# Fifteen short matmuls at the head of units in a one-core hybrid encoder layer

## The chip, the cores and the metric

The kernel runs on one core of a Trainium2 chip, all in float32 (matmul operands in the reduced form fp32r). The metric is the device time of one execution in microseconds. TensorE has two granted clock levels, 1.2 and 2.4 GHz.

## The reference

One layer of a chunk-causal encoder trunk on x (1, 256, 2048) and 256 memory tokens. Three residual sub-layers follow one another:

```python
x = x + hybrid_mixer(rmsnorm(x, norm_mix), w_in, ...)          # w_in: 2048 -> 14 parts
x = x + memory_cross_attention(rmsnorm(x, norm_xa), rmsnorm(mem, norm_mem), wq, wkv, wo, gq, gk)
x = x + conv_glu_ffn(rmsnorm(x, norm_ffn), w_up, w_conv, w_down)   # 2048 -> 2 x 5632 -> 2048

# hybrid_mixer:
(qkv_a, a_pre, b_pre, z_a, q_b, k_b, v_b, i_b, f_b, o_b, q_c, k_c, v_c, gate_pre) = split(h @ w_in)
y_a = gated_deltanet(...)      # 6 heads, chunks of 64
y_b = mlstm(...)               # 4 heads
y_c = stick_breaking(...)      # 6 heads
merged = gate_a * (y_a @ wb_a) + gate_b * (y_b @ wb_b) + gate_c * (y_c @ wb_c)
return merged @ w_out
```

Nearly all the work is products of the 256 tokens with weight matrices that are used once each.

## The kernel before

Every weight matrix is walked in units of 256 output columns by all 2048 input rows. STREAM names the phases and their number of units, in order: A 9, Z 3, GA 14, BQK 4, BV 2, BO 2, CQK 6, CV 3, GB 4, GC 6 (all from w_in), BR 8 (w_br), WO 8, K 8, Q 8, V 8, XO 8, UP 44, DN 32. A unit falls into two halves of 128 output columns; this text writes GC0.0 and GC0.1 for the first and second half of GC's first unit. A half is one accumulation over 16 steps of k.

For each half, SP loads the raw float32 weights, ACT splits off a high part into `w_hi_home` (line 547), DVE writes the remainder to `w_lo_home` (line 1139, in `lo_half`), and PE multiplies. Both weight tiles have two slots, one per half, so ACT may write the next high part of a half's slot when PE has finished with it (semaphore `half_used`), and PE may start a half when DVE has finished it (`lo_ready`). The activations stand in `x_hl` in the same way as a high and a low part; x_hl lies in `x_home`.

`three` (lines 1970 to 1972) is one step of k: high weights by high activations, high weights by low activations, low weights by high activations. Each of the three is a weight load of 128 x 128 and a matmul over 256 columns, all into one bank. A half of a phase that is feature-major (weights loaded, tokens moving) is 16 calls of it, 48 matmuls. BV, CV and V are token-major (TM_): the activations are loaded and the weights move, also 48 matmuls a half. UP takes another form (lines 2009 and 2011): a matmul over 512 columns and one over 256 in each step, and so does DN (lines 2485 and 2486).

The order of TensorE's work is written out by hand in one program. `half_unit` is a half with its waits, `product_half(m)` the half number m of the whole stream, `project(name)` a stretch of whole units (units 0 and 1 written out, the rest in a loop of pairs). Where the rest of the layer needs TensorE, its transposes and small products stand between two halves: between the halves of GA the DeltaNet's triangular solve and state, in CQK the mLSTM, in GB the stick-breaking attention, in WO3 transposes of the memory tokens (line 2053), in V the cross-attention. `norm_beside` runs eight halves and puts one product over 256 columns, with a tile of ones, in the middle of the fourth; it is called at WO4.0 and at K0.1. The first four halves of Q have such a product (line 2380) behind every second of them, up to Q3.1. The stretches from GC0.0 to WO2.1, from Q4.0 to Q7.1 and from XO1.0 to XO7.1 consist of halves alone. Every half's results go to columns of a bank that ACT or DVE then evacuate.

Of the kernel before, what the change touches and what calls it, by code (L numbers as in the profile page):

```python
# [8 lines left out]
P = 128  # L9
SEQ, D = 256, 2048  # L10
TT = SEQ // P
KC = D // P
# [10 lines left out]
BIG = 1e30  # L23
W_AT = 24
W_OF = {"UP": 0, "DN": 0, "V": 16}


def place_of(name):
    return W_OF.get(name, W_AT)

# [13 lines left out]
LEVELS, FIRST_LEVEL = 7, 4  # L44
BS = 1 << FIRST_LEVEL
BLOCKS = 12 * P // BS
FM, TM_, BR, DOWN = "feature-major", "token-major", "branches", "down"
# [15 lines left out]
FIRST, COUNT = {}, {}  # L63
# [62 lines left out]
def build_program(nc, T, out):  # L126
# [3 lines left out]
    with ctx:  # L130
# [8 lines left out]
        w_hi_home = sb("w_hi_home", [P, 2, KC * P + 64], f32r)  # L139
# [11 lines left out]
        x_hl = x_home[:, 8:8 + 2 * KC * SEQ].rearrange("p (j k s) -> p j k s", j=2, k=KC)  # L151
# [39 lines left out]
        y_hl = sb("y_hl", [P, 2, KC, SEQ], f32r, b_scope)  # L191
# [343 lines left out]
        def up_bank(par, half):  # L535

            return bank[4 + 2 * par + half]
# [1427 lines left out]
        def _(pe):  # L1965
            mm = nc.tensor.matmul

            def three(o, w, x, start, stop):
# [2 lines left out]
                mm(o, w[0], x[1], start=False, stop=False)  # L1971
                return mm(o, w[1], x[0], start=False, stop=stop)  # L1972

            def wait_bank(name, i):

                if isinstance(i, int) and i < 2:
                    u = FIRST[name] + i - 2
                    if u < 0:
                        return
                    before = phase_of(u)  # L1980
                    e, n = evacuated(before, u - FIRST[before])
                    pe.wait_ge(evac[e], n)
                else:
                    e, n = evacuated(name, 0)
                    pe.wait_ge(evac[e], i + (n - 2))

            def half_unit(name, i, par, hp, half, acts, ready=None, passed=None, parts=None, ks=range(KC)):

                kind = kind_of[name]
                whole = hp * 4 + (2 * par + half + 1)  # L1990
                pe.wait_ge(*((wp_l, parts) if parts else (lo_ready, whole)))
                if kind == TM_:
                    for k in range(KC // 2):
                        kk = half * (KC // 2) + k
                        at = place_of(name) + k * CW
                        w = [t[:, half, at:at + CW] for t in (w_hi_home, w_lo_home)]
                        for a in range(TT):
                            x = [acts[:, j, kk, a * P:(a + 1) * P] for j in range(2)]
                            last = three(bank[par + 2 * a][:, 0:CW], x, w, kk == 0, kk == KC - 1)
                else:  # L2000
                    cuts = (0, GH, GH + MH, KC) if kind == BR else (0, KC)
                    for k in range(KC if name == "UP" else 0):
                        if parts and k == KC // 2:
                            pe.wait_ge(lo_ready, whole)
                        if ready and k % ready[2] == 0:
                            pe.wait_ge(ready[0], ready[1] + k // ready[2] + 1)
                        o = up_bank(par, half)
                        at = place_of(name) + k * P
                        mm(o[:, :].rearrange("p (j s) -> p j s", j=2), w_hi_home[:, half, at:at + P], acts[:, :, k, :],  # L2009
                           start=k == 0, stop=False)  # L2010
                        last = mm(o[:, SEQ:2 * SEQ], w_lo_home[:, half, at:at + P], acts[:, 0, k, :], start=False, stop=k == KC - 1)  # L2011
                    for k in ks if name != "UP" else ():
                        if parts and k == KC // 2:
                            pe.wait_ge(lo_ready, whole)
                        if ready and k % ready[2] == 0:
                            pe.wait_ge(ready[0], ready[1] + k // ready[2] + 1)
                        g = sum(k >= c for c in cuts) - 1
                        w = [t[:, half, k * P:(k + 1) * P] for t in (w_hi, w_lo)]
                        last = three(bank[par + 2 * g][:, half * SEQ:(half + 1) * SEQ], w, [acts[:, j, k, :] for j in range(2)],
                                     k == cuts[g], k + 1 == cuts[g + 1])  # L2020
                        if kind == BR and half and k + 1 in cuts[1:3]:
                            last.then_inc(br_t, 1)
                        if passed is not None and k % 2 and k + 1 < KC:
                            last.then_inc(passed, 1)
                if ks[-1] == KC - 1:
                    last.then_inc(half_used, 1)

            def product_half(m, acts=x_hl, ready=None, passed=None, parts=None, ks=range(KC)):

                name, i, par, hp, half = half_of(m)  # L2030
                if half == 0 and ks[0] == 0:
                    wait_bank(name, i)
                half_unit(name, i, par, hp, half, acts, ready, passed, parts, ks)

            def project(name, acts, start=0, stop=None):
                def unit(i, par, hp):
                    wait_bank(name, i)
                    for half in range(2):
                        half_unit(name, i, par, hp, half, acts)

                stop = COUNT[name] if stop is None else stop
                if start < 2:
                    each_unit(pe, name, unit, start, min(2, stop))
                each_unit(pe, name, unit, max(2, start), stop)
# [10 lines left out]

            def norm_beside(k, m, acts):

                product_half(m, acts)
                product_half(m + 1, acts)
                product_half(m + 2, acts)  # L2060
                product_half(m + 3, acts, ks=range(KC // 2))
                pe.wait_ge(n_add, 5 * k)
                mm(bank[3][:, 0:SEQ], ones[:, :], tmp[:, 0, 0:SEQ], start=True, stop=True).then_inc(n_ss, 1)
                product_half(m + 3, acts, ks=range(KC // 2, KC))
                for j in range(4, 8):
                    product_half(m + j, acts)
# [67 lines left out]
            pe.wait_ge(gw_h, 2)  # L2134
            mm(bank[4][:, SEQ:2 * SEQ], fold, gate_sums[:, :], start=True, stop=True).then_inc(row_mm, 1)
            for m in range(4, 14):
                product_half(m)
            pe.wait_ge(row_v, ROW_V)
            for a in range(TT):
                nc.tensor.transpose(bank[5][:, a * P:(a + 1) * P], rt[:, a * P:(a + 1) * P], ident[:, :])  # L2140
# [49 lines left out]
            pe.wait_ge(qk_e, 6)  # L2190
            chunk_pairs(kk_t, bank[2:5], GH)
            product_half(m + 5)
            product_half(m + 6)
            m += 7
            for _ in range(2 * FIRST_LEVEL - 1):
                product_half(m)
                m += 1
            pe.wait_ge(rows, 160)
            for l in range(FIRST_LEVEL, LEVELS):
# [72 lines left out]
            for j in range(3):  # L2272
                to_features(bank[3 + j], j, lambda h, a: S_T[:, a * GH + h, :], y_t)

            for name in ("BQK", "BV", "BO"):
                project(name, x_hl)


            def scores(b, k, q):
# [67 lines left out]
            product_half(m + 7)  # L2347


            project("GC", x_hl)  # L2350
            pe.wait_ge(y_lo, 4)
            project("BR", y_hl)

            m = first_half("WO")
            product_half(m, x_hl, (m_lo, 0, 2))
# [101 lines left out]
            product_half(m, x_hl, (xo_l, 0, 2), ks=range(4, KC))  # L2457
            product_half(m + 1, x_hl)

            project("XO", x_hl, 1, COUNT["XO"] - 1)  # L2460
            m = first_half("UP")
            product_half(m - 2, x_hl)
            product_half(m - 1, x_hl, None, x_free)
# [75 lines left out]
```

## Time and profile before

| what | value |
|---|---|
| three runs | 1995.47, 2001.36, 2000.78 us (median 2000.78) |
| the profiled execution | 2001.66 us |
| its span in the profile | 1999.8 us, 34706 instructions |
| PE (matmuls) busy | 1985.7 us (99%) |
| PEld (weight loads) busy | 1895.3 us (95%) |
| DVE busy | 1216.7 us (61%) |
| ACT busy | 891.6 us (45%) |
| DMA, mean over the span | 191 GB/s |

The span runs from the first to the last instruction; the execution's own time is 1.9 us longer. Matmuls are pipelined: one matmul's record lasts longer than the step to the next, so the pitch is read from starts or from counts in a stretch, and busy time does not tell it. In a window a matmul that overlaps its edge is counted too.

### The profile page before, as it was taken

Reading aid. Unit: us, or ns where it says so; the run is one execution under the profiler, and the core shown is the slowest. Engines: PE = TensorE matmul, PEld = TensorE weight load, DVE = VectorE, ACT = ScalarE, POOL = GpSimd, SP = SyncE. Lnnn points to the kernel's source line nnn. Section 1 sums busy time; section 2 is a strip of 40 time slices with the busy share of each in tenths; the row PEclk is TensorE's granted clock in tenths of the full one; section 3 lists DMA queues with packets and bytes.
Section 4 is the critical chain, followed back from the end, with each engine's and each line's share of the span. In section 5 each row is a group of like instructions: output and inputs, shape, how many; then the busy total and the mean of one; then the engine's idle time right before and its main releaser. Section 6 shows DMA issues by size and latency. Waiting matters only on the chain.

```text
span 1999.8 us, 34706 instructions
## 1 busy us (share of the span) xinstructions
PE 1985.7 (99%) x14790; PEld 1895.3 (95%) x14790; DVE 1216.7 (61%) x1352; ACT 891.6 (45%) x877; POOL 40.3 (2%) x62
## 2 busy tenths in 40 slices
PE   8999999999999999999999999999999999999999
PEld 8999999999999999999999999888888888888888
DVE  5677645445454476676655345777777777754444
ACT  5445434434374333455434444544444444433333
POOL 1000100000000000000000000000000000000000
PEclk9999999999999999999999999999999999999999
DMA  8665744665557756565554455665656565567564
GB/s 268 212 200 196 226 159 143 211 198 169 181 167 267 238 190 217 177 196 170 191 187 127 151 165 190 214 207 173 204 174 204 175 202 176 176 205 223 185 203 134
DMA packets 356636, 382.65 MB, mean 191 GB/s; under 512 B 8143, under 2 KB 351603, under 8 KB 355123
## 3 DMA queue, kind: packets, MB, share of 16 engines
q1 hardware_dynamic: 350947, 353.36, 55.3%
q0 software_dynamic: 5584, 27.70, 3.9%
q8 instruction: 88, 1.44, 0.3%
q14 instruction: 17, 0.14, 0.0%
HBM read 367.47 MB, written 13.58 MB: 191 GB/s over the span
## 4 chain that ended last, share of the span: by engine, by line
PE 98%; DVE 1%; ACT 0%; DMA 0%; issue 0%; SPq 0%; DVEq 0%; ACTq 0%
PE bank L1970 19%; PE bank L1971 18%; PE bank L1972 18%; PE bank L2009 16%; PE bank L2011 8%; PE bank L2485 8%; PE bank L2486 4%; PE bank L2392 1%; PE bank L2411 1%; PE bank L2169 1%; DVE w_lo_home L1139 0%; PE bank L2215 0%; PE bank L2072 0%; PE bank L2163 0%; DMA ident<-in_shape_masks 0%; PE bank L2281 0%
## 5 line engine op out<-in xcount | busy, mean ns | idle before, releaser
L1139 DVE TENSOR_TENSOR w_lo_home<-raw,w_hi_home 128x2048 fp32r<-128x2048 f32 (+1 forms) x349 | 757.0, 2169 | 604.5 <-ACT w_hi_home L547 604.2
L547 ACT ACTIVATE w_hi_home<-raw 128x2048 fp32r<-128x2048 f32 (+2 forms) x359 | 644.8, 1797 | 1047.0 <-PE bank L1972 627.6
L1970 PE MATMUL bank<-x_home,w_hi_home 128*128 128x256 f32 x2304 | 648.8, 282 | 2.0 <-DVE w_lo_home L1139 1.9
L1972 PE MATMUL bank<-x_home,w_lo_home 128*128 128x256 f32 x2304 | 644.4, 280 | 0.0
L1971 PE MATMUL bank<-x_home,w_hi_home 128*128 128x256 f32 x2304 | 644.4, 280 | 0.0
L2009 PE MATMUL bank<-x_home,w_hi_home 128*128 128x512 f32 x1408 | 488.5, 390 | 0.1
L1970 PEld LDWEIGHTS bank<-x_home,w_hi_home 128*128 128x128 f32 x2304 | 435.1, 189 | 2.9 <-issue 1.4
L1972 PEld LDWEIGHTS bank<-x_home,w_lo_home 128*128 128x128 f32 x2304 | 437.0, 190 | 0.0
L1971 PEld LDWEIGHTS bank<-x_home,w_hi_home 128*128 128x128 f32 x2304 | 433.1, 188 | 0.2
L2011 PE MATMUL bank<-x_home,w_lo_home 128*128 128x256 f32 x1408 | 397.1, 282 | 0.0
L2009 PEld LDWEIGHTS bank<-x_home,w_hi_home 128*128 128x128 f32 x1408 | 264.2, 188 | 55.5 <-issue 0.4
L2011 PEld LDWEIGHTS bank<-x_home,w_lo_home 128*128 128x128 f32 x1408 | 266.5, 189 | 0.0
L2485 PE MATMUL bank<-act_hl,w_hi_home 128*128 128x512 f32 x704 | 245.1, 391 | 0.0
L2486 PE MATMUL bank<-act_hl,w_lo_home 128*128 128x256 f32 x704 | 198.5, 282 | 0.0
L2485 PEld LDWEIGHTS bank<-act_hl,w_hi_home 128*128 128x128 f32 x704 | 132.2, 188 | 27.5
L2486 PEld LDWEIGHTS bank<-act_hl,w_lo_home 128*128 128x128 f32 x704 | 133.2, 189 | 0.0
L1970 PE MATMUL bank<-w_hi_home,mem_hl 128*128 128x256 f32 x256 | 73.6, 287 | 0.0
L1874 DVE SCALAR_TENSOR_TENSOR tmp<-tmp,vec 128x254 f32<-128x254 f32 (+1 forms) x176 | 73.1, 478 | 0.0
L1970 PE MATMUL bank<-mem_hl,w_hi_home 128*128 128x256 f32 x256 | 72.2, 282 | 0.0
L1972 PE MATMUL bank<-mem_hl,w_lo_home 128*128 128x256 f32 x256 | 72.0, 281 | 0.0
L1971 PE MATMUL bank<-mem_hl,w_hi_home 128*128 128x256 f32 x256 | 72.0, 281 | 0.0
L1972 PE MATMUL bank<-y_hl,w_lo_home 128*128 128x256 f32 x256 | 72.0, 281 | 0.0
(315 smaller groups left out, 1946.4 us busy)
## 6 DMA issues: line engine op xcount, KB each, us to landing
raw<-in_w_in SPq DMA_DIRECT2D x52, 2048.0 KB, 8.5
raw<-in_ffn_up SPq DMA_DIRECT2D x44, 2048.0 KB, 7.9
raw<-in_ffn_down SPq DMA_DIRECT2D x32, 1408.0 KB, 6.9
raw<-in_xa_wkv SPq DMA_DIRECT2D x16, 2048.0 KB, 9.2
raw<-in_w_br SPq DMA_DIRECT2D x8, 2048.0 KB, 8.3
raw<-in_w_out SPq DMA_DIRECT2D x8, 2048.0 KB, 8.3
raw<-in_xa_wq SPq DMA_DIRECT2D x8, 2048.0 KB, 8.3
raw<-in_xa_wo SPq DMA_DIRECT2D x8, 2048.0 KB, 8.4
```

The source lines that it names most:

```text
L547: return nc.scalar.activation(out_, in_, func, **kw)
L1139: tt(split_out(w_lo, kind, half, at), halves(raw, kind, half, par), split_out(w_hi, kind, half, at).bitcast(f32), ALU.subtract).then_inc(l ...
L1874: ins = v.scalar_tensor_tensor(o, b, w, o, ALU.mult, ALU.add)
L1970: mm(o, w[0], x[0], start=start, stop=False)
L1971: mm(o, w[0], x[1], start=False, stop=False)
L1972: return mm(o, w[1], x[0], start=False, stop=stop)
L2009: mm(o[:, :].rearrange("p (j s) -> p j s", j=2), w_hi_home[:, half, at:at + P], acts[:, :, k, :], start=k == 0, stop=False)
L2011: last = mm(o[:, SEQ:2 * SEQ], w_lo_home[:, half, at:at + P], acts[:, 0, k, :], start=False, stop=k == KC - 1)
L2169: last = mm(o[:, i * P:(i + 1) * P], lhs(n), rhs(n), start=True, stop=True)
L2392: last = mm(mb(j)[:, 0:SEQ], qT[:, 4 * h + c, a * P:(a + 1) * P], kT[:, 4 * h + c, :], start=c == 0, stop=c == XC - 1)
L2485: mm(o[:, :].rearrange("p (j s) -> p j s", j=2), w_hi_home[:, half, at:at + P], x, start=g + k == 0, stop=False)
L2486: last = mm(o[:, SEQ:2 * SEQ], w_lo_home[:, half, at:at + P], x[:, 0, :], start=False, stop=g * DG + k == FC - 1)
```

## The change

`lead_in` is one extra matmul that starts and stops its own accumulation, with the half's own first weights and activations: with LEAD_WIDE 128 weight columns by 2 tokens, with LEAD_SMALL 4 weight columns by 16 tokens. It is issued behind the half's waits and writes columns of the half's own output, which the first real matmul of the half (start=True) then overwrites. SETTLE is the pair: wide at the head of a unit's first half, small at the head of its second. The pairs go to the units A4 (m = 8, 9), GA3 (m + 6, m + 7), GC0, BR0, WO4, K1 and XO1, and BO0 gets the small one at the head of its first half. Where `project` is now called twice, the order of the halves is as before.

```diff
+LEAD_WIDE, LEAD_SMALL = (P, 2), (4, 16)
+SETTLE = (LEAD_WIDE, LEAD_SMALL)
...
+            def lead_in(o, w, x, shape):
+                m, n = shape
+                return mm(o[0:m, 0:n], w[:, 0:m], x[:, 0:n], start=True, stop=True)
...
-            def half_unit(name, i, par, hp, half, acts, ready=None, passed=None, parts=None, ks=range(KC)):
+            def half_unit(name, i, par, hp, half, acts, ready=None, passed=None, parts=None, ks=range(KC), lead=None):
...
                     cuts = (0, GH, GH + MH, KC) if kind == BR else (0, KC)
+                    if lead:
+                        lead_in(up_bank(par, half)[:, 0:SEQ] if name == "UP" else bank[par][:, half * SEQ:(half + 1) * SEQ],
+                                w_hi_home[:, half, place_of(name):], acts[:, 0, 0, :], lead)
...
             def norm_beside(k, m, acts):
-                product_half(m, acts)
-                product_half(m + 1, acts)
-                product_half(m + 2, acts)
+                leads = dict(zip((m + m % 2, m + m % 2 + 1), SETTLE))
+                for j in range(3):
+                    product_half(m + j, acts, lead=leads.get(m + j))
...
             for m in range(4, 14):
-                product_half(m)
+                product_half(m, lead={8: LEAD_WIDE, 9: LEAD_SMALL}.get(m))
...
-            product_half(m + 6)
+            product_half(m + 6, lead=LEAD_WIDE)
             m += 7
-            for _ in range(2 * FIRST_LEVEL - 1):
-                product_half(m)
+            for j in range(2 * FIRST_LEVEL - 1):
+                product_half(m, lead=None if j else LEAD_SMALL)
...
-            for name in ("BQK", "BV", "BO"):
+            for name in ("BQK", "BV"):
                 project(name, x_hl)
+            project("BO", x_hl, 0, 1, leads=(LEAD_SMALL, None))
+            project("BO", x_hl, 1)
...
-            project("GC", x_hl)
+            project("GC", x_hl, 0, 1, leads=SETTLE)
+            project("GC", x_hl, 1)
             pe.wait_ge(y_lo, 4)
-            project("BR", y_hl)
+            project("BR", y_hl, 0, 1, leads=SETTLE)
+            project("BR", y_hl, 1)
...
-            project("XO", x_hl, 1, COUNT["XO"] - 1)
+            project("XO", x_hl, 1, 2, leads=SETTLE)
+            project("XO", x_hl, 2, COUNT["XO"] - 1)
```

## Rows read from the trace of the kernel before

**Rows 1.** The page: engines, clock in 40 slices, chain by engine, two costliest groups.

```profile
PE 1985.7 (99%) x14790; PEld 1895.3 (95%) x14790; DVE 1216.7 (61%) x1352; ACT 891.6 (45%) x877; POOL 40.3 (2%) x62
...
PEclk9999999999999999999999999999999999999999
...
PE 98%; DVE 1%; ACT 0%; DMA 0%; issue 0%; SPq 0%; DVEq 0%; ACTq 0%
...
L1139 DVE TENSOR_TENSOR w_lo_home<-raw,w_hi_home 128x2048 fp32r<-128x2048 f32 (+1 forms) x349 | 757.0, 2169 | 604.5 <-ACT w_hi_home L547 604.2
L547 ACT ACTIVATE w_hi_home<-raw 128x2048 fp32r<-128x2048 f32 (+2 forms) x359 | 644.8, 1797 | 1047.0 <-PE bank L1972 627.6
```

**Rows 2.** Windows, line 1970: stretch, its length, busy us (count), clock, DMA share, GB/s.

```profile
611.75:679.59 67.84, 53.97 (x192) 1.00 0.83 286
679.59:770.04 90.45, 71.97 (x256) 1.00 0.59 188
1179.62:1258.76 79.14, 62.97 (x224) 1.00 0.59 190
110.14:159.09 48.95, 39.77 (x144) 1.00 0.63 204
364.94:403.02 38.08, 30.93 (x112) 1.00 0.65 211
```

**Rows 3.** Lines, weight loads at 365, 612 and 1010 us: count, busy us, mean ns.

```profile
L1972 PEld LDWEIGHTS bank<-x_home,w_lo_home 128*128 128x128 f32 x112 | 21.0, 188 | 0.0
...
L1970 PEld LDWEIGHTS bank<-x_home,w_hi_home 128*128 128x128 f32 x192 | 36.9, 192 | 0.0
L1972 PEld LDWEIGHTS bank<-x_home,w_lo_home 128*128 128x128 f32 x192 | 36.1, 188 | 0.0
...
L1972 PEld LDWEIGHTS bank<-x_home,w_lo_home 128*128 128x128 f32 x102 | 19.6, 192 | 0.0
L1970 PEld LDWEIGHTS bank<-x_home,w_hi_home 128*128 128x128 f32 x102 | 19.2, 188 | 0.0
```

**Rows 4.** Timeline of PE around 424.8 us: start, length, line, operands.

```profile
424.67 0.28 PE L1972 MATMUL bank<-w_hi_home,x_home 128*128 128x256 f32 x1
424.78 0.28 PE L1970 MATMUL bank<-x_home,w_hi_home 128*128 128x256 f32 x1
424.90 0.28 PE L1971 MATMUL bank<-x_home,w_hi_home 128*128 128x256 f32 x1
```

**Rows 5.** Lines, line 1971 in GA0.0 (161), A7.0 (106), WO3.0 (807), WO3.1 (814 us).

```profile
L1971 PE MATMUL bank<-x_home,w_hi_home 128*128 128x256 f32 x15 | 4.1, 276 | 0.0
...
L1971 PE MATMUL bank<-x_home,w_hi_home 128*128 128x256 f32 x12 | 3.3, 276 | 0.0
...
L1971 PE MATMUL bank<-x_home,w_hi_home 128*128 128x256 f32 x14 | 3.9, 276 | 0.0
...
L1971 PE MATMUL bank<-x_home,w_hi_home 128*128 128x256 f32 x14 | 3.9, 281 | 0.0
```

**Rows 6.** Timeline of PE behind V0.1 and ahead of A7.0.

```profile
1058.51 0.94 PE L2386 MATMUL bank<-ones,tmp 128*128 128x1 f32 x8
1059.52 0.28 PE L1971 MATMUL bank<-w_lo_home,mem_hl 128*128 128x256 f32 x1
...
104.43 0.22 PE L2141 MATMUL bank<-ident,rt 4*128 4x4 f32 x1
104.80 0.28 PE L1971 MATMUL bank<-x_home,w_hi_home 128*128 128x256 f32 x1
```

**Rows 7.** Waits of PE from 224 to 232 us, and DVE's timeline there.

```profile
PE bank L1970 <- DVE w_lo_home L1139: 1.1, 1, 1.1
...
228.68 2.28 DVE L1139 TENSOR_TENSOR w_lo_home<-raw,w_hi_home 128x2048 fp32r<-128x2048 f32 x1
```

**Rows 8.** Windows of UP (line 2009) and DN (line 2485).

```profile
1291.20:1745.34 454.14, 454.14 (x1312) 1.00 0.58 187
...
1833.62:1855.81 22.19, 22.19 (x65) 1.00 0.62 189
```

More of the change, by code:

```diff
@@ L2026, in half_unit, with product_half @@
                     last.then_inc(half_used, 1)
-            def product_half(m, acts=x_hl, ready=None, passed=None, parts=None, ks=range(KC)):
+            def product_half(m, acts=x_hl, ready=None, passed=None, parts=None, ks=range(KC), lead=None):
                 name, i, par, hp, half = half_of(m)
@@ L2032, in product_half, with project @@
                     wait_bank(name, i)
-                half_unit(name, i, par, hp, half, acts, ready, passed, parts, ks)
-            def project(name, acts, start=0, stop=None):
+                half_unit(name, i, par, hp, half, acts, ready, passed, parts, ks, lead)
+            def project(name, acts, start=0, stop=None, leads=(None, None)):
                 def unit(i, par, hp):
@@ L2038, in unit @@
                     for half in range(2):
-                        half_unit(name, i, par, hp, half, acts)
+                        half_unit(name, i, par, hp, half, acts, lead=leads[half])
                 stop = COUNT[name] if stop is None else stop
```

## The prediction

> **What bounds the kernel now.** I read the engine busy times, the chain of waits, the windows by stretch, then the timeline around single places. TensorE's matmul row is busy 1985.7 of 1999.8 us, 98% of the chain of waits that ended last is PE, and the granted clock is 9 tenths or more in all 40 slices [rows 1], so it is the 2.4 GHz level throughout. The chain per half unit behind it has room: ACT's w_hi split (1.80 us mean) waits for PE, and DVE's w_lo split (2.17 us) waits for ACT [rows 1]; together they take 4.0 us where PE takes over 5.4 us for a half. So the time is the sum of TensorE's steps, and only their pitch or number can change it.
>
> The pitch is what the reader must see. A half unit is 16 steps of k with three matmuls each, one of them on line 1970, so the count of that line times three gives all. Windows that are whole halves [rows 2]: 611.75 to 679.59 is 67.84 us for 192 x 3 = 576 matmuls, 117.8 ns each; 364.94 to 403.02 is 38.08 us for 112 x 3 = 336, 113.3 ns; 110.14 to 159.09 is 48.95/432 = 113.3 ns. Same instructions, same shapes, same clock, two speeds. Per half unit: 48 x 117.8 = 5.654 us against 48 x 113.3 = 5.440 us, a difference of 0.214 us. The weight loads say the same: in the fast stretch all three take 188 ns, in the other two exactly one of the three takes 192, the one of line 1970 at 611 us and the one of line 1972 at 1010 us [rows 3]. So there is one arrangement with the 113 ns pitch and at least two with 118.
>
> An arrangement holds until something else is put into the stream. From 600 to 803 us nothing but half units runs and the pitch stays slow for 36 halves; through the wait of 1.1 us at 229 us it stays slow too. At 424.78 us, where token-major BV ends and feature-major BO begins with no instruction between, it goes from 113 to 118 ns in one step [rows 4]. Products in between re-draw it: I went over every place before 1047 us where transposes or small products stand between halves. Of 16 met in the fast arrangement 11 came out fast and 5 slow; of 22 met slow, 6 came out fast. The rows show the first of the 11, a change to fast behind the 4-column transposes of line 2141, and WO3, where the same 16 transposes turn slow to fast and, one half later, fast to slow (mean 276 ns is fast, 281 slow) [rows 5]. None of the 7 lone 256-column products met slow (as the one in WO5.1) turned it fast.
>
> **The change, part by part.** It adds 15 short matmuls with their weight loads (two each in A4, GA3, GC0, BR0, WO4, K1 and XO1, one in BO0) and removes or moves nothing: splitting a stretch's first unit off leaves the same order. All stand behind waits that the half unit has anyway, and write columns that the next real matmul starts afresh, so no wait, DMA or queue is added.
>
> Cost: the trace has no such pair. From above: the eight one-column products with full weight loads of line 2386 start at 1058.51, the second matmul behind them at 1059.52 [rows 6]: 1.01 us, less one ordinary step of 0.118, is 0.892 us or 0.112 us each. From further: from the last 4-column transpose at 104.43 to the second matmul at 104.80 are 0.37 us, 0.255 above one step. Below, nothing: a short load may hide in the step beside it. I take 0.112, since it is the row with both a full load and a short stream: 15 x 0.112 = 1.7 us, bounds 0 and 3.8 us.
>
> Gain, if wide and then small leave the fast arrangement. I count the halves that are slow now, from the second lead on:
> - A4.1 to A6.1: 5 halves, 1.07 us.
> - GA3.1 to GA6.1: 7 halves. The first four lie before the stall where PE waits 1.1 us for DVE's w_lo, which is queued behind the row recurrence on DVE until 228.68 us [rows 7]; an earlier PE waits longer there, so only three count: 0.64 us (1.50 without the stall, 0 at worst).
> - BO0.0 to BO1.1 and CQK0.0: 5 halves, 1.07 us (0 if the later mLSTM waits on DVE keep their times; those are released by scores that PE itself brings forward, so I keep it).
> - GC0.1 through BR to WO2.1: 33 halves, 7.06 us, the largest term. Nothing is inserted here but BR's own pair.
> - WO4.1 to K0.1: 9 halves, 1.93 us. K1.1 to Q7.1: 29 halves, 6.21 us.
> - XO1.1 to XO7.1: 13 halves, 2.78 us.
>
> Sum 20.8 us. DMA can follow: the fast stretch at 365 us already moves weights at this pace with 0.65 share [rows 2]. Less the leads: 19.1. In WO, K and Q other products follow the leads (in the middle of WO5.1 and K2.0, and behind four halves of Q): 6.5 + 27.5 = 34 halves, 7.28 us. With the trace's own share of fast arrangements lost at an insertion, 5 of 16, I take off 2.3 us. Left: 16.8 us. V, whose weights and moving operands are exchanged, I count at nothing (15 halves at about 116.6 ns by the timeline: up to 2.4 us more).
>
> UP and DN I also count at nothing. UP's pairs of a 512- and a 256-column matmul take 454.14 us for 1310 pairs (two of the 1312 overlap the edges), 346.7 ns; DN's 22.19/64 = 346.7 [rows 8]. Only one speed shows there, behind every transpose of DN too.
>
> The profiled execution took 2001.66 us, 0.9 above the median of the three runs shown. 2001.66 - 16.8 = 1984.9 us is the forecast. Its own range is 1978 (nothing lost at insertions, V faster) to 1991.
>
> The Trainium skill, "TensorE: Matmul & The Clock Gate", section "Part 2: What happens when you issue a matmul", speaks against all this: the weight load and the moving operand have separate read ports into the array, so loading the next weights takes nothing from the running matmul. By that rule the pitch has no arrangement to be moved out of, and the change is its own 1.7 us. The trace disagrees so far: one load in three takes 4 ns more exactly where the pitch is 4.5 ns longer [rows 2, 3].
>
> **The rivals.**
> - Nothing settles. The leads act as most lone products did: 7 of 7 left a slow stream slow. For: those 7, and that a stream comes back to its own rhythm within a few steps. Against: the 4-column case, and 6 of 22 overall. Time 2001.66 + 1.7 = 2003.4. Chance 0.20.
> - It works from one of the slow arrangements alone [rows 3]. If only where line 1970's load is long (GC, BR, BO): 8.1 - 1.7 = 6.4, so 1995.3. If only where line 1972's is long (A, GA, WO, K, XO): 12.6 - 2.3 - 1.7 = 8.6, so 1993.1. Chance 0.14.
> - Slower: the leads in A and GA pass on another arrangement, and the draw at GA10.1 (310 us), which turned fast in this trace, turns slow. Everything from there to CV2.1 is fast now (36 halves without BO and CQK0.0), and would lose 36 x 0.214 = 7.7 us, and the other leads fail: 2001.66 + 7.7 + 1.7 = 2011. It needs both; if GC and BR alone flip (7.1 us), it is a draw. For: the draws from GA7 to GA10.1 alternate with what came before (slow, slow, fast, slow, fast, slow, slow, fast). Chance 0.10.
> - UP and DN carry over. A pair's 346.7 ns may itself be a slow arrangement: XO then hands UP a fast stream, and if a pair loses the 13.4 ns that a triple loses (3 x 117.8 - 3 x 113.3), 2112 pairs give 28 us more: 1957. Against: not one of 2112 pairs ever ran so, though transposes re-drew eight times. Chance 0.04.
> - The forecast: 0.52.
>
> **How the numbers follow.** One run in three of before came out at 1995.47, 5 us under the others, about 25 halves at the other speed; so what an insertion leaves may differ from run to run, which widens all cases by some us. A measurement of this kernel tells about 0.3%, 6 us, from no change. Faster by more than that: 0.50 of the forecast's 0.52, 0.09 of the half-working case, 0.04: 0.63. Slower: the third rival, and a little of the first with an unlucky draw: 0.12. Within: 0.25. For 8 in 10 the range must take in the forecast, the half-working case and most of "nothing settles", whose upper bound is 2001.66 + 3.8 = 2005.5: 1978 to 2004.
>
> **What would show it.** In the changed profile GC, BR, WO0 to WO2 should run at 113.3 ns (5.44 us a half) with three loads of 188 ns; each of the seven stretches is its own test, as is BO. The DVE wait at GA5.1 should grow to about 1.9 us. If GC is fast and BR slow, the pair destroys what it finds fast. The prediction is wrong if GC to WO2 stays at 117.8, or if UP's pairs leave 346.7.

## The result, and the profile after

| | before | changed |
|---|---|---|
| runs, us | 1995.47, 2001.36, 2000.78, 2000.53 | 1989.79, 1987.00, 1985.33, 1986.17 |
| median | 2000.65 | 1986.59 |
| the profiled execution (its span) | 2001.66 (1999.8) | 1989.79 (1987.8) |

The ratio is 0.9938, 95% interval 0.9917 to 0.9958: faster by 12.4 us, between 8.4 and 16.6. The forecast was 1984.9 in a range of 1978 to 2004; the mechanism held, two of its terms (A and BO) came to nothing, the largest (GC to WO2) gave 5.2 us of its 7.1, and part of the agreement is luck, told below. The profiled execution of the changed kernel was the longest of its four.

In the profile's lines everything behind line 27 has moved: 1974 to 1976 are now the three products of a step (before: 1970 to 1972), 1981 is the lead, 2021 and 2023 are UP's pair (2009 and 2011), 1143 and 551 the DVE and ACT splits (1139 and 547). The page of the changed kernel first: the same engines, the same clock, 15 matmuls more.

```profile
PE 1972.4 (99%) x14805; PEld 1880.9 (95%) x14805; DVE 1216.3 (61%) x1352; ACT 892.2 (45%) x877; POOL 40.3 (2%) x62
PEclk9999999999999999999999999999999999999999
PE 96%; DVE 2%; DMA 1%; ACT 1%; issue 0%; SPq 0%; DVEq 0%; ACTq 0%
```

These answer to [rows 1]. PE is busy 13.3 us less with more instructions: nothing was taken away from it, its steps became shorter.

The windows of line 1974, whole stretches of halves (stretch, its length, busy us and count, clock, DMA share, GB/s), answer to [rows 2]; one matmul in three is counted, so the pitch is length / (3 x count), less one where the count is one over a multiple of 16:

```profile
76.00:98.55 22.55, 17.92 (x64) 1.00 0.71 222
425.40:448.09 22.69, 18.07 (x64) 1.00 0.60 188
522.22:550.49 28.27, 22.40 (x80) 1.00 0.51 158
625.36:658.00 32.64, 26.50 (x97) 1.00 0.98 350
692.05:762.77 70.72, 57.41 (x208) 1.00 0.57 182
889.04:943.49 54.45, 44.20 (x160) 1.00 0.65 193
1181.43:1241.27 59.84, 48.58 (x176) 1.00 0.56 180
```

625.36 to 658.00 is six halves of GC in 32.64 us, 113.3 ns; 692.05 to 762.77 thirteen halves of BR in 70.72 us, 113.3 ns; K (889) and XO (1181) the same. But A5 to A6 (76 us) and BO (425 us) stay at 117.8, and so does CV (522 us: 28.27 us for five halves of 16), which the kernel before ran at 113.3. Where BR is fast, its three loads take 188 ns, as in the 365 us stretch of [rows 3]; in BO it is now the second product's load that takes 192:

```profile
L1974 PEld LDWEIGHTS bank<-y_hl,w_hi_home 128*128 128x128 f32 x209 | 39.2, 188 | 0.0
L1975 PEld LDWEIGHTS bank<-y_hl,w_hi_home 128*128 128x128 f32 x208 | 39.0, 188 | 0.0
L1976 PEld LDWEIGHTS bank<-y_hl,w_lo_home 128*128 128x128 f32 x208 | 39.0, 188 | 0.0
...
L1975 PEld LDWEIGHTS bank<-x_home,w_hi_home 128*128 128x128 f32 x63 | 12.1, 192 | 0.0
L1974 PEld LDWEIGHTS bank<-x_home,w_hi_home 128*128 128x128 f32 x63 | 11.8, 188 | 0.0
```

I call the arrangements F (all loads 188 ns, pitch 113.3) and A, B, C by which product's load takes 192: the first, the second or the third of a step (pitch 117.8 in all three). These names hold where the weights are loaded. In the token-major phases the loads do not tell: CV ran at 117.8 ns with none of its loads at 192,

```profile
L1974 PEld LDWEIGHTS bank<-w_hi_home,x_home 128*128 128x128 f32 x80 | 15.0, 188 | 0.0
L1975 PEld LDWEIGHTS bank<-w_lo_home,x_home 128*128 128x128 f32 x80 | 15.0, 187 | 0.0
```

and V runs at 116.6 to 117.8 ns with loads of 188 in every profile. There only the pitch itself tells. The kernel before had C in A2 to A6, GA3, WO4 to Q7 and XO, and A in BO and GC to WO2; both profiles of it agree on all of these.

The leads in the timeline of PE and its weight loads, the wide one at GA3.0 and the small one at GA3.1 (start, length, line):

```profile
202.14 0.19 PEld L1981 LDWEIGHTS bank<-x_home,w_hi_home 128*128 128x128 f32 x1
202.26 0.17 PE L1981 MATMUL bank<-x_home,w_hi_home 128*128 128x2 f32 x1
202.49 0.28 PE L1975 MATMUL bank<-x_home,w_hi_home 128*128 128x256 f32 x1
...
207.91 0.08 PEld L1981 LDWEIGHTS bank<-x_home,w_hi_home 128*4 128x4 f32 x1
208.02 0.17 PE L1981 MATMUL bank<-x_home,w_hi_home 128*4 128x16 f32 x1
208.25 0.28 PE L1975 MATMUL bank<-x_home,w_hi_home 128*128 128x256 f32 x1
208.37 0.28 PE L1976 MATMUL bank<-x_home,w_lo_home 128*128 128x256 f32 x1
208.48 0.28 PE L1974 MATMUL bank<-x_home,w_hi_home 128*128 128x256 f32 x1
```

Each costs the same: from the lead's start to the second real product 0.23 us, where one ordinary step is 0.118, so 0.11 us (at A4.0 alone, behind a wait, these are 0.31 us). Behind the small one the steps are 0.12, then 0.11: the stream is at its shorter pitch three matmuls later. The small load takes 84 to 88 ns against 188 for 128 columns. The Trainium skill, "TensorE: Matmul & The Clock Gate", section "LDWEIGHTS (loading the stationary operand)", puts the load at its number of columns over 1.2 GHz; an estimate from it is 103 ns less for 124 columns fewer, and the trace agrees within the spread (188 - 84 = 104). The rule's own figures, 107 and 3 ns, are some 81 ns under both records; there the measurement decides.

Where the time went, by the start of the first real matmul of a half in the two profiles:

| half | before, us | changed, us | shift |
|---|---|---|---|
| A4.0 | 69.81 | 70.28 | +0.47 |
| A7.0 | 104.58 | 104.97 | +0.39 |
| GA3.0 | 201.48 | 202.28 | +0.80 |
| GA5.1 | 231.02 | 231.62 | +0.60 |
| BO0.0 | 424.78 | 425.40 | +0.62 |
| CQK0.1 | 454.28 | 454.98 | +0.70 |
| GB0.0 | 557.24 | 560.24 | +3.00 |
| GC0.0 | 611.75 | 614.04 | +2.29 |
| WO3.0 | 805.63 | 803.05 | -2.58 |
| K1.0 | 875.54 | 871.84 | -3.70 |
| V0.0 | 1047.31 | 1037.79 | -9.52 |
| XO1.0 | 1179.62 | 1170.14 | -9.48 |
| XO7.1 | 1253.11 | 1241.27 | -11.84 |

The span ends 12.0 us earlier. The gain comes from GC to Q and XO alone. CQK to CV gives 2.3 us away: CQK1.0, CQK4.0 to CQK5.1 and CV, 11 halves x 0.214 us, ran at 117.8 ns in this execution. They begin behind waits, told below.

The waits of the changed kernel ahead of GC5.0, from 664 to 671 us (who waited for whom: us in total, times, longest):

```profile
ACT w_hi_home L551 <- DMA raw<-in_w_in: 4.7, 1, 4.7
DVE w_lo_home L1143 <- ACT w_hi_home L551: 4.8, 1, 4.8
PE bank L1974 <- DVE w_lo_home L1143: 0.7, 1, 0.7
...
PE bank L1974 <- DVE w_lo_home L1143: 1.6, 1, 1.6
```

The first group is new: in GC's last units the raw weights land too late, ACT waits 4.7 us for them, DVE for ACT, and PE 0.7 us at the end, at the head of GC5.0. The window from 625 to 658 us points to the reason: the DMA engines are at 0.98 share and 350 GB/s. The kernel before was as full in the middle of GC, though its mean over all of GC is 0.83 [rows 2]; its window of line 1970 there:

```profile
620.00:654.00 34.00, 27.07 (x97) 1.00 0.97 342
```

So a faster PE had next to nothing to draw on. In the seven of the 13 profiles in which GC ran fast, the step into GC5.0 took 0.82 to 1.04 us; in the six others 0.12 to 0.15. The second group is GA5.1, where PE waited 1.1 us before and 1.6 now [rows 7].

### The profile page after: what moved, and what is told of

It reads as the page before. It is cut to its first block, busy times and chain, and to the rows that moved or that the text cites. A ratio compares the mean times of both kernels' runs of the same rounds, so it can differ in the third digit from the quotient of the medians.

```text
span 1987.8 us, 34736 instructions
## 1 busy us (share of the span) xinstructions
PE 1972.4 (99%) x14805; PEld 1880.9 (95%) x14805; DVE 1216.3 (61%) x1352; ACT 892.2 (45%) x877; POOL 40.3 (2%) x62
## 4 chain that ended last, share of the span: by engine, by line
PE 96%; DVE 2%; DMA 1%; ACT 1%; issue 0%; SPq 0%; DVEq 0%; ACTq 0%
PE bank L1974 18%; PE bank L1976 18%; PE bank L1975 18%; PE bank L2021 16%; PE bank L2023 9%; PE bank L2502 8%; PE bank L2503 4%; DVE w_lo_home L1143 1%; PE bank L2408 1%; PE bank L2427 1%; DMA raw<-in_w_in 1%; PE bank L2181 1%; ACT w_hi_home L551 0%; PE bank L2227 0%; PE bank L2089 0%
## 5 line engine op out<-in xcount | busy, mean ns | idle before, releaser
L1974 PE MATMUL bank<-w_hi_home,mem_hl 128*128 128x256 f32 x256 | 73.5, 287 | 0.0
L1975 PE MATMUL bank<-w_lo_home,mem_hl 128*128 128x256 f32 x256 | 71.5, 279 | 0.0
L1976 PE MATMUL bank<-w_hi_home,mem_hl 128*128 128x256 f32 x256 | 71.4, 279 | 0.0
L1974 PE MATMUL bank<-mem_hl,w_hi_home 128*128 128x256 f32 x256 | 71.2, 278 | 0.0
L1974 PE MATMUL bank<-y_hl,w_hi_home 128*128 128x256 f32 x256 | 70.9, 277 | 0.0
```

The costliest lines, as they stand in the source:

```text
L1974: mm(o, w[0], x[0], start=start, stop=False)
```

## The experiments

Three theories stood against each other: (1) every lead re-draws the arrangement in a way that depends on its shape and on what it meets; (2) any inserted matmul gives a stream one more chance of about a third; (3) the place alone does it, whatever the shape. Each run but the last two, which repeat the two kernels, is the changed kernel with the edit shown. The half units were read one by one from the profiles. A table of all at the end counts them.

**Wide leads alone.**

```diff
-SETTLE = (LEAD_WIDE, LEAD_SMALL)
+SETTLE = (LEAD_WIDE, None)
...
-                product_half(m, lead={8: LEAD_WIDE, 9: LEAD_SMALL}.get(m))
+                product_half(m, lead={8: LEAD_WIDE}.get(m))
...
-                product_half(m, lead=None if j else LEAD_SMALL)
+                product_half(m, lead=None)
...
-            project("BO", x_hl, 0, 1, leads=(LEAD_SMALL, None))
+            project("BO", x_hl, 0, 1, leads=(LEAD_WIDE, None))
```

> Only the wide lead (128 weight columns by 2 tokens) stays, at the head of the first half of each of the seven units and of BO0; no small one. Theory 1 (each lead is its own re-draw, and on a slow stream the wide one only shifts which of the three loads is long, as in the changed kernel at GA3, GC0, BR0, WO4, K1 and XO1): these six stretches stay at 117.8 ns, only A4 may become fast; 1999 to 2002 us. Theory 2 (any inserted matmul gives the stream one more chance of about a third): two or three of the stretches become fast, 1993 to 1998 us. Theory 3 (the place of the lead does it, not its shape): six become fast, about 1986 us.

1994.38 us, median of ten; ratio to before 0.9990, interval 0.9979 to 1.0001: no difference that is clear of the noise. (The 26 runs of before beside this one and the next three spread from 1993.54 to 2002.29 us, median 1999.58.) The windows of six halves of GC and the loads there:

```profile
620.18:654.10 33.92, 26.98 (x97) 1.00 0.96 340
...
L1976 PEld LDWEIGHTS bank<-x_home,w_lo_home 128*128 128x128 f32 x58 | 11.1, 192 | 0.0
L1974 PEld LDWEIGHTS bank<-x_home,w_hi_home 128*128 128x128 f32 x57 | 10.7, 188 | 0.0
```

33.92 us for 96 x 3 matmuls (one of the 97 is at the edge) is 117.8 ns, and the third product's load is the long one: the lead met A and left C. At GA3, WO4 and XO1 it met C and left B. None of the four became fast, so theory 3 is out. K1.0 and BR0.0 (GC5.0 had turned fast behind a pause at 665.29 us) were met in F and left A. A4, which starts behind a wait, came out F.

The time is under the 1999 to 2002 us that I expected, and the profiled execution was at 1992.54. It has 102 halves in F where the first profile of before has 53, and most of them lie where no lead stands. A window in K, from K2.1 to K3.1:

```profile
889.12:905.44 16.32, 13.25 (x48) 1.00 0.70 217
```

16.32 us for 48 x 3 matmuls is 113.3 ns. The stream turned at the lone 256-column products in the middle of WO5.1, met in B, and of K2.0, met in A; in the kernel before both are met in C, and stay. The wide leads had only changed what these products met. In the trace such a lone product is two matmuls of 378 ns, so it is not the same as one more matmul of the stream. I counted this one kind of insertion over all 13 profiles (WO5.1, K2.0, and ahead of Q1.0 to Q4.0): from A to F 12 of 12, from B to F 1 of 1, from C to C 18 of 18, from F to F 47 of 47. The prediction's "none of the 7 lone products met slow turned it fast" rests on C: in the kernel before the six that I count here all meet C. The seventh, ahead of A2.0, looks the same in the trace (128 x 128 by 256, two matmuls of 377 ns), is met in A and took A to C in all 13 profiles. So for these products the shape and what it meets do not decide alone; what differs there isn't shown.

**Small leads alone.**

```diff
-SETTLE = (LEAD_WIDE, LEAD_SMALL)
+SETTLE = (None, LEAD_SMALL)
...
-                product_half(m, lead={8: LEAD_WIDE, 9: LEAD_SMALL}.get(m))
+                product_half(m, lead={9: LEAD_SMALL}.get(m))
...
-            product_half(m + 6, lead=LEAD_WIDE)
+            product_half(m + 6)
```

> Only the small lead (4 weight columns by 16 tokens) stays, half a unit into the seven units and at BO0. Theory 1: it turns a slow stream fast from whichever of the three slow arrangements, so the wide one is not needed: GA, GC, BR, WO, K, XO at 113.3 ns from their second half, A too since it is met slow; 1984 to 1988 us. But where BR and K are met fast it may turn them slow, which would cost 22 halves in BR to WO2 (4.7 us) and up to 29 in K and Q (6.2 us): then 1991 to 1997 us. Theory 2 (chance of a third at each place): 1993 to 1998 us.

1988.53 us, median of five; ratio 0.9954, interval 0.9939 to 0.9969.

```profile
624.79:657.43 32.64, 26.50 (x96) 1.00 0.99 351
1180.88:1240.72 59.84, 48.58 (x177) 1.00 0.57 181
```

Six halves of GC in 32.64 us, eleven of XO in 59.84: 113.3 ns each. The small lead turned C (GA, XO) and A (GC, BR) to F without a wide one. Where it met F, at A4.1, WO4.1 and K1.1, it left A. So it is a switch, not a repair, and that is what the wide lead is for: it takes F to A, so that the small one behind it never meets F. WO and K lost little all the same, because the lone products in WO5.1 and K2.0 turned A back to F. The re-draws are no lottery: theory 2 is out.

**Leads of full length.**

```diff
-LEAD_WIDE, LEAD_SMALL = (P, 2), (4, 16)
+LEAD_WIDE, LEAD_SMALL = (P, SEQ), (P, SEQ)
```

> The same 15 places, but every lead is an ordinary product, 128 weight columns by 256 tokens, also overwritten. It costs 15 x 0.118 = 1.8 us. Theory 1 (shortness matters, since a matmul of full length keeps the stream's rhythm): no stretch changes its arrangement, 2002 to 2003 us. Theory 2 (any insertion is a re-draw): some become fast, 1990 to 1997 us.

1996.11 us, median of ten; ratio 0.9982, interval 0.9970 to 0.9995. The loads in GC, from 630 to 650 us:

```profile
L1975 PEld LDWEIGHTS bank<-x_home,w_hi_home 128*128 128x128 f32 x57 | 10.9, 192 | 0.0
L1976 PEld LDWEIGHTS bank<-x_home,w_lo_home 128*128 128x128 f32 x58 | 10.9, 188 | 0.0
```

GC went A to C to B: an inserted full-length matmul takes one place in the period of three, so the long load falls on the product before, and the pitch stays 117.8. The same at GA3, A4.1, BR0, K1 and XO1; at WO4, met in F, it stayed F. No lead of this kind turned a slow stream fast. The profile has 83 halves in F all the same, 30 more than before: WO3.1 to WO7.1, because these leads leave F alone, and Q, because the lone products in K2.0 and at Q1.0 met A. Thirty halves are 6.4 us, less 1.8 for the leads; the median stands 3.5 us (0.2%) under before.

The step into K4.0 shows how little re-draws. The timeline of PE there (start, length, line; the end of K3.1, which is fast, the place, and K4.0, which is slow):

```profile
908.00 0.28 PE L1975 MATMUL bank<-mem_hl,w_hi_home 128*128 128x256 f32 x1
908.11 0.28 PE L1976 MATMUL bank<-mem_hl,w_lo_home 128*128 128x256 f32 x1
908.23 0.31 PE L1974 MATMUL bank<-mem_hl,w_hi_home 128*128 128x256 f32 x1
908.38 0.28 PE L1975 MATMUL bank<-mem_hl,w_hi_home 128*128 128x256 f32 x1
908.49 0.28 PE L1976 MATMUL bank<-mem_hl,w_lo_home 128*128 128x256 f32 x1
908.61 0.28 PE L1974 MATMUL bank<-mem_hl,w_hi_home 128*128 128x256 f32 x1
908.73 0.28 PE L1975 MATMUL bank<-mem_hl,w_hi_home 128*128 128x256 f32 x1
908.85 0.28 PE L1976 MATMUL bank<-mem_hl,w_lo_home 128*128 128x256 f32 x1
```

Up to 908.23 the starts are 0.11 to 0.12 apart, 113 ns in the mean; one step takes 0.15; behind it they are 0.12 apart, 118 in the mean. A pause of 0.035 us took F to A. The place is the same each time: all ten profiles that came to K4.0 in F have one long step behind its first matmul, of 142 to 151 ns, and the three that came in C have none. Four of the ten left in A (148, 149, 149 and 149 ns); six stayed in F (142 to 145 ns, and 151 once). What makes the pause isn't shown.

**The pair in the other order.**

```diff
-LEAD_WIDE, LEAD_SMALL = (P, 2), (4, 16)
+LEAD_WIDE, LEAD_SMALL = (4, 16), (P, 2)
```

> The pair in the other order: small first, wide half a unit later (BO0 gets the wide one). Theory 1: the small one makes the stream fast for half a unit, the wide one meets it fast. If a lead on a fast stream turns it slow, as the small one did at A4.1, the stretches end slow: 1999 to 2003 us. If the wide one leaves a fast stream fast: 1985 to 1989 us. Theory 3 (two short matmuls in any order): 1986 us.

1999.42 us, median of ten; ratio 0.9998, interval 0.9985 to 1.0011. The six halves of GC:

```profile
620.77:654.69 33.92, 26.98 (x97) 1.00 0.97 342
```

GC0.0 was F (the small lead met A), and from GC0.1 on all was A. The same at GA3, BR0, WO4 and XO1. WO5.1's lone product then took A to F, K's small lead met F and left A, the wide one took A to C, and from there K and Q stayed in C. The gain of the leads hangs on their order.

**Leads in UP.**

```diff
-            project("UP", x_hl, 1)
+            project("UP", x_hl, 1, 2, leads=SETTLE)
+            project("UP", x_hl, 2, 3, leads=SETTLE[::-1])
+            project("UP", x_hl, 3)
```

> The changed kernel with four leads more, in the feed-forward phase: wide and small at the heads of UP1.0 and UP1.1, small and wide at UP2.0 and UP2.1. Theory 1 (UP's pairs of a 512- and a 256-column matmul have one arrangement): the pairs stay at 346.7 ns throughout, 0.4 us longer than the changed kernel, about 1987 to 1990 us. Rival (UP and DN sit in a slow arrangement too): from UP1.1 or UP2.0 on the pairs take about 333 ns, through UP alone 18 us less, with DN 28 us: 1959 to 1969 us.

1989.04 us, one run. The windows of line 2021 behind the four leads:

```profile
1291.63:1308.27 16.64, 16.64 (x49) 1.00 0.45 144
```

16.64 us for 48 pairs (one of the 49 at the edge), 346.7 ns as in [rows 8], and so through UP and DN. In none of the 13 profiles does a pair follow the one before in under 343 ns, whichever of F, A, B and C the halves of XO ahead of them were in. Leads of both shapes in both orders, and in the changed kernel a fast XO ahead of it, left UP as it was. The rival that UP and DN are in a slow arrangement too found nothing for it; another shape of lead was not tried.

**What of the small lead does it: 128 columns by 16 tokens, 4 by 2, 4 by 256.** Three runs, each with one number changed, the wide lead ahead as it was:

```diff
-LEAD_WIDE, LEAD_SMALL = (P, 2), (4, 16)
+LEAD_WIDE, LEAD_SMALL = (P, 2), (P, 16)
...
+LEAD_WIDE, LEAD_SMALL = (P, 2), (4, 2)
...
+LEAD_WIDE, LEAD_SMALL = (P, 2), (4, SEQ)
```

> The small lead gets 128 weight columns and keeps 16 tokens (wide stays 128 by 2 ahead of it). If the short weight load (4 columns) is what turns a slow stream fast, GA3.1, GC0.1, BR0.1, WO4.1, K1.1 and XO1.1 stay at 117.8 ns: 1997 to 2002 us. If the number of tokens is what matters, all six are fast as in the changed kernel: 1985 to 1990 us.

> The small lead keeps its 4 weight columns and gets 2 tokens instead of 16. If the short weight load is what turns a slow stream fast, the six second halves are fast: 1985 to 1990 us. If it needs the longer stream of 16 tokens, they stay slow: 1997 to 2002 us.

> The small lead keeps its 4 weight columns and gets 256 tokens, the length of every other matmul. If the short weight load alone decides, the six second halves are fast: 1985 to 1991 us. If the matmul must be short as well, so that the next load is not held to the stream's rhythm, they stay slow, as behind the full-length pair: 1996 to 2002 us.

One run each: 1994.82, 1987.80 and 1988.36 us, beside 2000.62 of before. The six halves of GC in the three:

```profile
622.34:656.26 33.92, 26.98 (x96) 1.00 0.97 339
```

```profile
622.50:655.14 32.64, 26.50 (x96) 1.00 0.98 350
```

```profile
621.44:654.08 32.64, 26.50 (x96) 1.00 0.99 349
```

With 4 columns GC is fast whatever the number of tokens, 2 or 256, and so are GA3.1, BR0.1, K1.1 and XO1.1. The short weight load does it. With 128 columns and 16 tokens my expectation failed in both its forms: three of the six were fast (GA3.1, K1.1, XO1.1) and three slow. The wide lead had left B ahead of those three leads, and A or C ahead of the others. A lead with 128 columns and a short stream has a rule of its own, which its use as the first of the pair had hidden: B goes to F.

**Leads placed by that table.**

```diff
-                product_half(m, lead={8: LEAD_WIDE, 9: LEAD_SMALL}.get(m))
+                product_half(m, lead={9: LEAD_WIDE, 10: LEAD_SMALL}.get(m))
...
-            product_half(m + 6, lead=LEAD_WIDE)
+            product_half(m + 6, lead=LEAD_SMALL)
...
-                product_half(m, lead=None if j else LEAD_SMALL)
+                product_half(m)
...
-            project("BO", x_hl, 0, 1, leads=(LEAD_SMALL, None))
+            project("BO", x_hl, 0, 1, leads=(None, LEAD_SMALL))
...
-            product_half(m + 7)
+            product_half(m + 7, lead=LEAD_SMALL)
...
-            project("GC", x_hl, 0, 1, leads=SETTLE)
+            project("GC", x_hl, 0, 1)
...
-            product_half(m + 1, x_hl)
+            product_half(m + 1, x_hl, lead=LEAD_SMALL)
...
-            project("XO", x_hl, 1, 2, leads=SETTLE)
+            project("XO", x_hl, 1, 2)
```

> Leads placed by what each did in the runs so far: a stream that is always met slow gets the small lead alone (GA3.0, GB3.1 instead of GC0, BO0.1 instead of BO0.0, XO0.1 instead of XO1), and A's pair moves one half later (A4.1, A5.0), away from the wait ahead of A4.0. BR, WO and K keep their pairs. If the table holds, these halves are fast: A5.0 to A6.1, GA3.0, BO0.1 to CQK0.0, GB3.1 to GC0.1, XO0.1 to XO1.0. That is 4 + 4 + 3 + 2 halves or 13 x 0.214 = 2.8 us (GA3.0 is lost in the wait at GA5.1), and 3 leads fewer give 0.3 us: about 3 us under the changed kernel, 1983 to 1984.5 us. If the response depends on the place and not on the arrangement met, BO0.1, GB3.1 and XO0.1 stay slow and the stretches behind them too: 1989 us or more.

1985.74 us, median of five (1985.47 to 1988.58); ratio to before 0.9936, interval 0.9922 to 0.9951. The windows of BO0.1 to CQK0.0, GB3.1 to GC0.1 and XO0.1 to XO1.0:

```profile
429.03:450.80 21.77, 17.72 (x64) 1.00 0.62 194
605.53:621.96 16.43, 13.35 (x48) 1.00 0.58 194
1163.80:1174.78 10.98, 8.92 (x32) 1.00 0.60 191
```

The first is 64 x 3 matmuls in 21.77 us, the second 48 x 3 in 16.43, the third 32 x 3 in 10.98: 113 to 114 ns with their leads, fast. In the profile every half named in the expectation was F. The gain of 3 us didn't come out: CQK0.1, which follows an insertion and was F in every profile that met it slow, was met fast here and came out A; CQK4.0 behind its wait came out A and kept CV slow; WO4, met in B, was turned to F by the wide lead and to A by the small one.

**The changed kernel again, beside it.** No edit.

> The changed kernel again, on the chip and beside the runs of the one above. Both theories: 1985 to 1989 us, with GA3.1, GC0.1, BR0.1, XO1.1 fast in the profile and A4.1 and BO0.0 slow; halves behind a wait (GA5.1, CQK1.0, CQK4.0, GC5.0) come out either way.

1987.21 us, median of five (1986.09 to 1988.68); ratio 0.9943, interval 0.9928 to 0.9957. The version above is 1.5 us under it in the median, and their runs and intervals overlap: I can't call it faster. The windows of A4.1 to A6.1 and of CQK5 to CV2:

```profile
76.00:98.20 22.20, 18.04 (x66) 1.00 0.72 221
516.00:551.00 35.00, 28.43 (x103) 1.00 0.65 205
```

Both are fast here (22.20/198 and 35.00/309 us are 112 and 113 ns, with the matmuls at the edges), both were slow in the first profile of the same program. A4.0, behind its wait, came out B instead of F, and the small lead then turned B to F; CQK4.0 stayed F. This profile's span is 1984.4 us, 3.4 shorter than the first.

**The kernel before again.** No edit.

> The kernel before once more. Its executions lie between 1993.5 and 2002.3 us. If waits re-draw the arrangement, this profile differs from the first one only in stretches that begin behind a wait or behind other work that follows one (A4 to A6, GA0 to GA2, GA5.1 to GA7, CQK1.0, CQK4.0 to GB1), and GB3 to WO2 and WO4 to Q7 stay at 117.8 ns wherever no wait stands in them.

2001.89 us, one run. It differs from the first profile in A0.1 to A1.0, GA0.1 to GA1.1, the arrangement of GA2.0, and CQK1.0; these are behind waits or behind insertions that follow one. GC to WO2 and WO4 to Q7 were at 117.8 again. I didn't catch one of the 1994 us runs in a profile, so which stretch makes them isn't shown.

**All leads of the 13 profiles together** (the two of before have none), less the 9 at A4.0, which follow a wait (the wide one there left F five times and B twice), and the 10 at BO0.0, where the operands change places (nine left B whatever their shape, 128 x 256 left C; with no lead it is A in all three profiles):

| lead (columns x tokens) | met F | met A | met B | met C |
|---|---|---|---|---|
| 4 x 16 or 4 x 2 | to A, 9 of 9 | to F, 17 of 17 | to F, 10 of 10 | to F, 13 of 13 |
| 4 x 256 | to F, 1 of 1 | not met | to F, 3 of 3 | to F, 3 of 3 |
| 128 x 2 or 128 x 16 | to A, 22 of 22 | to C, 14 of 14 | to F, 6 of 6 | to B, 18 of 18 |
| 128 x 256 | to F, 2 of 2 | to C, 2 of 2 | to A, 4 of 4 | to B, 5 of 5 |

That is 129 leads, and none of them broke its rule. The pair of the change follows from it: from C the wide lead leaves B and the small one F, from A it is C and F, from F it is A and F. From B it is F and A, and the pair fails; WO4 met B in the run with UP's leads, in the one with 4 x 2 and in the one placed by the table, and failed in all three.

## Why the prediction was right

- **One fast and several slow arrangements, held until something is put in.** Right; three arrangements have the longer pitch. But I also said that it holds through a wait, from the one at GA5.1, which left the pitch alone (it took C to A). Waits re-draw: in the changed kernel's first profile GA5.1, CQK1.0 and CQK4.0 went from F to a slow arrangement behind a wait with nothing inserted, and in the second GA5.1 and CQK4.0 did not. That is why 2.3 us were lost in CQK and CV in one profile of the changed kernel and 0.2 in the other. In all, 21 halves are fast in the second alone (A4.1 to A6.1 and GA5.1 to GA6.1 among them) and 9 in the first alone (GB0.0 to GB1.1 among them); the 12 between are 2.6 us of the 3.4 between the spans, and 0.9 lies ahead of A2.0. Whether it also makes the 1995.47 us run of before, which I put to insertions, isn't shown. And the slow arrangements are not equal: a lone product turns A and B fast and leaves C, which I had read as a rule for all.
- **The leads leave F.** Right, in six of the seven stretches, for the reason given at even odds only: I had a tally of 6 in 22 and one case with 4 columns. The runs show a fixed rule. What decides is the 4-column weight load.
- **15 leads x 0.112 = 1.7 us.** Measured 0.110 to 0.111 each by the starts, the same for both shapes, but for the one at A4.0.
- **GC to WO2: 7.06 us.** The profile shows 4.87 us from GC0.0 to WO3.0, 5.2 with the three leads inside added back. Missing are the slow half BR0.0 (0.21) and new waits: 0.96 in the first two steps of GC5.0 for raw weights, 0.34 in WO0.0, at the step where the program waits for the last of the merged activations, and 0.19 at WO2.0; some 0.15 are the lead of GC0.0 and the steps behind the leads. I had taken DMA as able to follow from the 365 us stretch at 0.65 share; the share in GC was 0.83, and already 0.97 in its middle in the kernel before. This is the term that was mis-sized most.
- **K and Q 6.21, WO4 to K0 1.93, XO 2.78 us.** Measured 6.0 (K1.0 to V0.0), 1.3 (WO3.0 to K1.0) and 2.7 (XO1.0 to the end), each with the two leads in it added back; WO7.1 drew C behind a wait of 0.14 us. The 2.3 us that I took off for arrangements lost at the inner products were not lost: all 34 halves but WO7.1 stayed F, and the single products in WO5.1, K2.0 and Q left F alone.
- **A 1.07 us.** Wrong in this profile: the wide lead at A4.0 left F and the small one turned F to A. In the second profile A4.0 was B and A was gained. It stands behind a wait, and which it is differs from run to run.
- **BO 1.07 us.** Wrong in all profiles. BO0.0 is where the loaded and the moving operands change places; a small lead there left B (A without one). Half a unit later it works, as the leads placed by the table showed.
- **GA 0.64 us.** Half wrong. The wait at GA5.1 grew from 1.1 to 1.6 us (I said about 1.9) and left 0.3 us of the four halves ahead of it (GA3.0 to GA5.1 is 0.20 us shorter, with a lead of 0.11 in it). The three halves behind it, the ones that I had counted, came out in A; in the second profile they were F.
- **UP, DN and V nothing.** Right: UP's pairs at 346.7 ns, V's shift 0.04 us.
- **The separate read ports of the Trainium skill ("TensorE: Matmul & The Clock Gate", "Part 2: What happens when you issue a matmul").** The consequence that I drew from them, that the pitch can't be moved and the change costs its own 1.7 us, is refuted: the changed kernel is 12.4 us faster, and leads moved the arrangement in every profile that has them; whether the 4 ns on one load come from reading is not shown.

The balance: A, BO, GA, GC, WO, K and XO gave 5.2 us less than I had put down (1.07 + 1.07 + 0.34 + 1.86 + 0.6 + 0.2 + 0.1), CQK to CV took 2.3, and the discount of 2.3 wasn't needed. The last two cancel, so 16.8 - 5.2 = 11.6, and the profiled execution is 11.9 us under the one of before. The median of the four runs is 3.2 us lower still, and so came within 1.7 us of the forecast by luck with CQK to CV as much as by the working.

Open: what makes one load in three 4 ns longer, and why three slow orders lock in. The runs tell which input leads where, not the mechanism. Between 4 and 128 weight columns no lead was tried, so how short the load must be isn't shown.

## What to carry to other kernels

A stream of weight loads and matmuls that is bound by nothing but itself can run at more than one pitch, here 113.3 or 117.8 ns, and counts in a stretch show it, not the busy time. The durations of the loads by position show it too, but not in the token-major phases. Count before adding anything: if one position's load is longer throughout, an inserted matmul with a short weight load, here of 4 columns, can bring the stream to the shorter pitch for 0.11 us, and as the same insertion spoils a stream that is already fast, put one ahead of it that makes the input known. Put it behind an unbroken stretch and not behind a wait or at a change of operands, and look at what the shorter pitch then runs into: here new waits took a fifth of the largest gain.

## What the runs showed of the hardware that was not expected

- A longer load in the lead costs nothing more: 84 ns or 188, both leads lengthen the stream by 0.11 us.
- The insertion's effect is a fixed map of four arrangements, over the 129 leads of the table and 78 lone products without an exception (it does not cover A4.0 and BO0.0, nor the product ahead of A2.0, which took A to C 13 times of 13); a full-length matmul shifts the long load by one position, 128 columns with 2 or 16 tokens do the same in A and C but take B to F and F to A.
- Waits re-draw the arrangement, not every one, but a pause of 0.035 us can do it: at K4.0 in the run of full-length leads and in the ones with 128 x 16, with 4 x 256 and placed by the table, a single step of 148 to 149 ns took F to A. The same place has a step of 142 to 151 ns in the six other profiles that came to it in F, and there it changed nothing.
- UP's and DN's pair of 512 and 256 columns shows one pitch, 346.7 ns, behind every lead tried and every arrangement of XO.
- A stream can be slow with no long load in it: CV at 117.8 ns with loads of 187 and 188, V at 116.6 to 117.8 with loads of 188.
